# A gather of expert rows by one list of indices, and by two lists of which the second leaves out picks of weight zero

## The reference, cut to what matters

```python
PEER_TOPK = 16
...
        eidx = jnp.take_along_axis(cand_idx, pos, axis=-1)
        g = jax.nn.softmax(best, axis=-1)
        u = jnp.take(expert_u, eidx, axis=0)
        h = jax.nn.gelu(jnp.einsum('thkd,td->thk', u, xb))
        vv = jnp.take(expert_v, eidx, axis=0)
        return jnp.einsum('thk,thkd->td', (g * h.astype(jnp.float32)).astype(xb.dtype), vv)
```

## Time and profile before

| | |
|---|---|
| median of 3 runs | 3214.2 us (3211.79 to 3214.63) |
| span of the profiled execution, first to last instruction | 3210.9 us |
| instructions | 43682 |
| read from HBM | 1051.58 MB, 332 GB/s over the span |
| first gather starts | at 1816.18 us |
| last gather starts | at 3175.11 us |
| start of the last store | at 3205.95 us |

### The profile page before, as it was taken

One profiled execution on the slowest core, in us unless ns is written; L12 is line 12 of the kernel. 1 busy time (PEld: TensorE's weight loads), 2 busy tenths in 40 slices (PEclk: granted clock), 3 DMA queues, 4 the chain that ended last, 5 costly groups with the idle time before them and its releaser, 6 DMA issues.

```text
span 3210.9 us, 43682 instructions
## 1 busy us (share of the span) xinstructions
PE 2530.9 (79%) x17242; PEld 1248.3 (39%) x17242; DVE 1564.1 (49%) x3391; ACT 1048.7 (33%) x2457; POOL 581.5 (18%) x535
## 2 busy tenths in 40 slices
PE   8999988797988878878879878897778655555655
PEld 6677774484322222222228634343324211111111
DVE  4655655763100100100107466678675777777764
ACT  2533443521000000000006354577344444343433
POOL 0000000000000000000000143344443444444442
PEclk9999998998999999999999989898888777788778
DMA  4211302249999999999995499999999999999997
GB/s 152 101 58 66 122 26 112 92 158 382 427 427 427 427 427 427 427 427 427 427 411 195 176 418 399 417 418 383 420 419 420 420 420 419 420 419 420 420 419 331
DMA packets 128670, 1067.80 MB, mean 333 GB/s; under 512 B 14289, under 2 KB 17233, under 8 KB 27601
## 3 DMA queue, kind: packets, MB, share of 16 engines
q0 software_dynamic: 75456, 543.20, 41.0%
q1 hardware_dynamic: 53008, 521.81, 39.4%
HBM read 1051.58 MB, written 13.37 MB: 332 GB/s over the span
## 4 chain that ended last, share of the span: by engine, by line
DMA 50%; PE 34%; DVE 7%; ACT 6%; issue 2%; POOL 1%; ACTq 0%; DVEq 0%; SPq 0%; POOLq 0%
PE ps L92 33%; DMA gb<-in_peer_uv,eidx 27%; DMA gw<-in_eu 14%; DMA gw<-in_ed 8%; DVE gb L146 2%; PE ps L97 2%; ACT L168 1%; ACT dots L168 1%; ACT diag L168 1%; ACT prob L168 1%; POOL gb L86 1%; DVE prob L146 0%; DVE w_lo L115 0%; ACT prob_t L168 0%; DVE prob L120 0%
## 5 line engine op out<-in xcount | busy, mean ns | idle before, releaser
L92 PE MATMUL ps<-gb,diag 64*64 64x512 f32 x4096 | 662.0, 759 | 410.3 <-ACT diag L168 396.8
L146 DVE CUSTOM_DVE_ANT_0 gb<-gb,xn 128x1024 f32<-128x1024 f32 x512 | 627.1, 1225 | 378.5 <-DMA gb<-in_peer_uv,eidx 378.0
L86 POOL DMA_INDIRECT gb<-in_peer_uv,eidx x512 | 570.3, 1114 | 1312.6 <-PE ps L92 718.5
L92 PEld LDWEIGHTS ps<-gb,diag 64*64 64x64 f32 x4096 | 148.2, 155 | 847.6 <-ACT diag L168 746.3
L168 ACT ACTIVATE dots<-dots 128x1 f32<-128x1 f32 (+1 forms) x382 | 77.6, 203 | 618.3 <-DVE dots L146 611.5
L115 DVE TENSOR_TENSOR expert_act<-expert_act,ps 128x512 f32<-128x512 f32 x32 | 22.0, 687 | 523.8 <-PE ps L92 523.2
L92 PE MATMUL ps<-ga,xt 128*64 128x512 f32 x1024 | 229.2, 596 | 41.3 <-DMA ga<-in_eu 32.6
L92 PE MATMUL ps<-gw,xt 128*64 128x512 f32 x992 | 224.3, 601 | 25.4 <-DMA gw<-in_eu 16.2
L168 ACT ACTIVATE diag<-cons,dots 128x128 f32<-128x128 f32 x512 | 205.5, 401 | 41.1 <-ACT dots L168 0.4
L115 DVE TENSOR_TENSOR x<-x,ps 128x512 f32<-128x512 f32 (+1 forms) x96 | 61.4, 643 | 296.5 <-PE ps L92 294.9
L168 ACT ACT_TABLE_LOAD x124 | 159.1, 1283 | 8.1 <-PEq L3241 0.7
(11 more groups left out here) (360 smaller groups left out, 3616.9 us busy)
## 6 DMA issues: line engine op xcount, KB each, us to landing
ga<-in_eu SPq DMA_DIRECT2D x47, 2048.0 KB, 35.5
gw<-in_eg SPq DMA_DIRECT2D x46, 2048.0 KB, 30.7
ring<-in_wt SPq DMA_DIRECT2D x75, 1024.0 KB, 6.0
gw<-in_ed SPq DMA_DIRECT2D x32, 2048.0 KB, 35.5
ga<-in_ed SPq DMA_DIRECT2D x32, 2048.0 KB, 36.1
ga<-in_eg SPq DMA_DIRECT2D x17, 2048.0 KB, 32.2
gw<-in_eu SPq DMA_DIRECT2D x16, 2048.0 KB, 35.5
p_scratch<-spill SPq DMA_DIRECT2D x35, 256.0 KB, 2.1
```

Source lines behind the costliest of these rows:

```text
L86: self.e.indirect_dma_start(out, None, table, bass.IndirectOffsetOnAxis(ap=idx, axis=0)).then_inc(s, 16)
L92: i = self.e.matmul(out, l, r, start=st, stop=sp, skip_group_check=True)
L146: self.done(self.e.tensor_tensor_reduce(out=o, in0=a, in1=b, scale=scale, scalar=start, op0=o0, op1=o1, accum_out=acc), name)
```

## The change

Rows 256 to 495 are now of two kinds. A row is **whole**, as before, where n % 4 is 0 or 2 and n is not 256 or 384. The other 122 rows are **split**: a first gather fetches only u (4 KB for each partition) from the table seen as 32768 rows of 1024 floats, and a second one fetches only v, with an index that is known after the dot. 113 of the 122 second gathers have an upper bound on the index: DVE adds 65536 to the index of a pick whose dot is -11 or less, and the gather skips indices above 32767. DVE also sets the softmax weight of such a pick to zero, so what lies in the buffer does not count. The first nine second gathers (rows 256 to 271, quads 64 to 67) fetch all.

- The unit of the order is a **quad** of four rows, n = 4g to 4g + 3. After the four dots of a quad come (event "k") three small DVE instructions, `far`, `v_idx` and `mask`, then one gelu of four columns on ACT.
- POOL's order is: the u or whole gathers of quad g + 1 (four), then the v gathers of quad g (two), and so on.
- The sums of a quad's whole rows come during the dots of the next quad, the sums of its split rows one quad later (`sums_after`). "out" and "add" follow the order of the sums.
- Nine buffers are cut in halves: a u half is free after its dot, a v half after its sum. Four buffers (`KEPT`) are for whole rows. From row 496 on (`TAIL`) the 13 buffers are whole again.
- For blocks 2 and 3 the indices are doubled (`dv.ts(sif, siu, 2.0, MUL)`) and halved again for whole rows, one more small DVE instruction for each of 16 heads.

```diff
@@ Engine.gather
-        self.e.indirect_dma_start(out, None, table, bass.IndirectOffsetOnAxis(ap=idx, axis=0)).then_inc(s, 16)
+        if last is None:
+            self.e.indirect_dma_start(out, None, table, at).then_inc(s, 16)
+        else:
+            self.e.indirect_dma_start(out, None, table, at, bounds_check=last, oob_is_err=False).then_inc(s, 16)
@@ block_program
+    STEPS, GROW, ADD_LAG, HALVED, WHOLE, LAST = 27, 244, 2, 256, 496, 504
+    NO_GELU, FAR = -11.0, 65536.0
+    halves = I["peer_uv"].rearrange("e (t d) -> (e t) d", t=2)
+    def whole(n):
+        return n < HALVED or n % 4 in (0, 2) and n % 128 != 0 or n >= WHOLE
...
+    KEEP = sorted(range(len(ROW_BUFFERS)), key=lambda s: first_last[s])[:4]
+    PAIRED = [s for s in range(len(ROW_BUFFERS)) if s not in KEEP]
...
+    def sums_after(n):
+        if n < HALVED:
+            return list(row_group(n)) if n == row_group(n)[-1] else []
+        if n >= LAST:
+            k = n - LAST
+            return [[500, 501], [502, 503], [504, 505], [506, 507]][k] if k < 4 else [n]
+        g, j = n // 4, n % 4
+        before = [m for m in quad(g - 1) if whole(m)] if g > HALVED // 4 else []
+        later = [m for m in quad(g - 2) if not whole(m)] if g > HALVED // 4 + 1 else []
+        todo = later + before if g % 32 == 1 or g > WHOLE // 4 else before + later
+        return todo[j * len(todo) // 4:(j + 1) * len(todo) // 4]
@@ peer_order
+            yield ("u", n)
+            if n == group[-1]:
+                yield ("k", group)
+            for m in sums_after(n):
+                yield ("w", m)
+                q = SUM_AT[m]
+                if q == LAST - 1 or q % 128 == 127 and q < LAST:
+                    yield ("out", q // 128)
+                if 127 < q < LAST and q % 128 == ADD_LAG:
+                    yield ("add", q // 128 - 1)
@@ dv_peer
+            elif ev[0] == "k" and HALVED <= ev[1][0] < WHOLE:
...
+                if gated(n // 4):
+                    s4 = soft[:, i % 2, k:k + 4]
+                    dv.wait_ge(("inv", i, k // 16))
+                    dv.ts(far, d, NO_GELU, ALU.is_le, FAR, MUL)
+                    dv.stt(e, far, 1.0, e, ADD, ADD, name=("v_idx", n // 4))
+                    dv.stt(s4, d, NO_GELU, s4, ALU.is_gt, MUL, name=("mask", n // 4))
@@ po_peer
+        def v_row(n):
+            i, k = n // 128, n % 128
+            s, freed, _ = V_AT[n]
+            po.wait_ge(("v_idx", n // 4))
+            po.wait_ge(freed)
+            po.gather(v_of(n), halves, eidx[i % 2][:, k:k + 1], f"gv{s}", ("v_row", n), 2 * 16384 - 1 if gated(n // 4) else None)
+        for n in range(HALVED + 4):
+            u_row(n)
+        for g in range(HALVED // 4, WHOLE // 4):
+            for n in quad(g + 1):
+                u_row(n)
+            for n in quad(g):
+                if not whole(n):
+                    v_row(n)
+        for n in range(WHOLE + 4, 512):
+            u_row(n)
```

More of the change, by code:

```diff
@@ new lines, in quad, with places @@
+    def quad(g):
+        return range(4 * g, 4 * g + 4)
+    def places(rows, pieces, end, start=None):
+        held, out = list(start or [None] * len(pieces)), {}
+        for n in rows:
+            s = min((held[s] is not None, held[s] if held[s] is not None else s, s)
+                    for s, (_, first, _) in enumerate(pieces) if n >= first)[2]
+            freed = pieces[s][2] if held[s] is None else ("sum", held[s]) if held[s] < HALVED else (end, held[s])
+            out[n] = (s, freed, held[s] is None or held[s] < HALVED)
+            held[s] = n
+        return out, held
@@ new lines, in block_program @@
+    FIRST_AT, first_last = places(range(HALVED), ROW_BUFFERS, "sum")
+    KEEP = sorted(range(len(ROW_BUFFERS)), key=lambda s: first_last[s])[:4]
+    PAIRED = [s for s in range(len(ROW_BUFFERS)) if s not in KEEP]
+    KEPT = [(ROW_BUFFERS[s][0], 0, None) for s in KEEP]
+    U_PIECES = [(ROW_BUFFERS[s][0][:, 0:1024], 0, None) for s in PAIRED]
+    V_PIECES = [(ROW_BUFFERS[s][0][:, 1024:2048], 0, None) for s in PAIRED]
+    SPLIT = [n for n in range(512) if not whole(n)]
+    U_AT, u_last = places(SPLIT, U_PIECES, "dot", [first_last[s] for s in PAIRED])
@@ new lines, in u_of, with v_of, gated @@
+    def u_of(n):
+        return row_at(n)[0][:, 0:1024] if whole(n) else U_PIECES[U_AT[n][0]][0]
+    def v_of(n):
+        return row_at(n)[0][:, 1024:2048] if whole(n) else V_PIECES[V_AT[n][0]][0]
+    def gated(g):
+        return HALVED // 4 <= g < WHOLE // 4 and not any(V_AT[n][2] for n in quad(g) if not whole(n))
+    def row_group(n):
+        if n < GROW or n >= LAST:
+            return (n,)
+        if n < HALVED:
+            return (n - n % 2, n - n % 2 + 1)
+        return tuple(quad(n // 4))
@@ L2786, in peer_order @@
+    SUMS = [m for n in range(512) for m in sums_after(n)]
+    assert sorted(SUMS) == list(range(512)) and all(a // 128 <= b // 128 for a, b in zip(SUMS, SUMS[1:]))
+    SUM_AT = {m: q for q, m in enumerate(SUMS)}
+    ROW_ENDS = [SUMS[127], SUMS[255], SUMS[383], LAST - 1]
+    assert SUMS[LAST - 1] == LAST - 1
     def peer_order():
@@ L2810, in peer_order @@
                 done += 1
[L2811 to L2819, removed]
+            yield ("u", n)
[8 more added lines that the diff above has]
+                    yield ("add", q // 128 - 1)
+                if q == LAST + ADD_LAG:
+                    yield ("add", 3)
             if n - 3 in pass_rows:
```

148 lines of the change are left out of this document (88 added, 60 removed).

## The result

| | before | changed |
|---|---|---|
| median | 3213.6 us (3211.8 to 3214.6) | 3238.7 us (3235.2 to 3247.6) |
| ratio, 95% interval | 1 | **1.0083** (1.0068 to 1.0097) |
| span of the profiled execution | 3210.9 us | 3236.3 us |
| bytes in the DMA queues | 1067.8 MB | 1042.1 MB |

The change makes the kernel 0.8% slower (both measured again, on one chip). The forecast was 3196 us and faster; the range of 3176 to 3240 holds the result at its upper end.

The account below looks back on a forecast made before the run. DMA was taken to bound the kernel, with POOL next. Quads -38.6, block changes +15.6, first quads +0.7 and end +4.0 sum to -18.3 us: span 3192.6, time 3196 us; range 3176 to 3240.

Parts of the forecast that it names:

- The bound before: Before the change, the gathers' DMA queue sets the pace: 9.99 us per four rows, about ten gathers always queued.
- The saving in bytes, and the floor: In 56 bounded quads, 6282 skipped picks (26 MB) bring DMA's floor from 9.99 to 9.06 us, worth 52 us.
- the third rival: A skipped pick costs the engines as much as a fetched one: 10.15 us a quad, 3243 us; chance 0.07.
- POOL: Gathers begun in a dot wait for its end; quad taken as 9.3 us, between 9.06 and 9.64, gaining 38.6 us.
- The 9.64 us of the rival: POOL sets the quad's pace, each of four dots holding one gather 0.55 us: 3215 us; chance 0.19.
- the 78% that I set as its sign: If POOL leads, it is over 78% busy in the middle of block 2, with hardly any wait for DVE.
- There is slack, but of 1.4 us: After a quad's last u lands, the next whole row's bytes can begin at 8.9 us; the queue runs dry at 10.3.
- The two changes of block: Rows 266 and 394 wait for buffers whose sums stand behind the add; DMA stalls 2 x 7.8 = 15.6 us.
- The end: Block 3's "out" comes at row 505, not 503, with eight sums behind it: 4 us later (0 to 5).
- The slower rival: Bounded gathers take 0.2 us more each on POOL, which is the bound: 10.04 us a quad, 3237 us; chance 0.21.
- The fourth rival: Dots are also held by gathers, 0.47 us each: with the choice's long steps 9.6 us a quad, 3213 us; chance 0.03.
- What was to show it: Signs in the trace: 26 MB less read, GB/s and POOL's share in block 2, gather means, stalls near rows 266 and 394.

Follow-up runs that it names:

- b1: Kernel before the change, with dots of rows 256 on over 512 of 1024 columns: 3214.9 us, ratio 1.0000 to the kernel before.
- e7b: Changed kernel with five whole-row buffers, early add, dots over 512 columns from row 256 and threshold -7.8: 3167.0 us, 0.9848 of the kernel before.
- e8: Changed kernel with five whole-row buffers and early add, all picks of the bounded gathers fetched (FAR = 0): 3223.8 us, 1.0028 of the kernel before.
- e3: Changed kernel with five whole-row buffers instead of four, and the add at a new block's first sum instead of third: 3185.1 us, 0.9915 of the kernel before.
- e9: Changed kernel with five whole-row buffers and early add, all picks of the 113 bounded gathers skipped: 3177.5 us, 0.9889 of the kernel before.
- e5b: Changed kernel with five whole-row buffers instead of four, add left at the third sum: 3194.2 us, 0.9936 of the kernel before.
- e1: Changed kernel with FAR = 0, so all picks of the bounded gathers are fetched: 3247.3 us, 1.0104 of the kernel before.

## Why the prediction was wrong

- **The bound before.** Right: the gathers' queue led, and short dots gave nothing (b1). The quad was 10.12 us by the dots' starts, not 9.99, or 0.12 more; the rate of the window (420 GB/s) counts the small transfers of the other queue too.
- **The saving in bytes, and the floor.** Right. 25.7 MB of 26, and all 6282 picks; the floor of 9.06 us a quad was measured at 9.15 to 9.26 (e7b), and a quad with all fetched in six gathers at 10.19 (e8) where the third rival's sum had 10.15. One bound is off in the sums: a quad of 9.5 us gives 3207 us, not 3209.
- **POOL.** The mechanism was right, and the value chosen wrong. A gather that begins in a dot ends after it, by 0.81 to 0.82 us without a bound and 0.87 with one. In the changed kernel 150 of the 288 gathers of 2600 to 3100 us begin in a dot, before it was 85 of 197, and the means are 1.20 and 1.17 us, not the 1.10 of the earlier trace rows that pulled my choice towards the floor. 6 x (1.19 + 0.30) = 8.9 us are POOL's own. The 9.64 us of the rival (7.44 without any meeting, and four holds of 0.55) came close to what a kernel led by POOL takes, 9.48 in e3 and 9.50 in e9 over the 50 quads, but partly by luck: in e3 the holds come to 1.5 us and not 2.2, and waits of 0.5, which the sum did not have, make up for them. In e3 POOL was busy 76% of the time, so the 78% that I set as its sign was too high.
- **The failed step: "There is slack, but of 1.4 us".** The chain from dots to gathers was counted from the dots to the v gathers and "then the first whole row", as if that row's buffer were free. It was not: with four buffers for whole rows POOL waited for their sums, about 1 us per quad, and in series with the holds. 8.9 + 1.0 + 0.3 = 10.2 us instead of 9.3. I had named this place ("it is used up when ...") but only for the rare steps, Exp's table and the choice, and took the way from a dot's end to the release from the earlier trace rows, 2.5 us; in the changed kernel the sum alone ended 5.4 us (median) after the last dot. The index to POOL's gather, 0.8 us at the least, was put at nothing too. The 50 measured quads were to give 34.5 us (0.69 each) and cost 3.4, which is 37.9 of the 43.7 us between forecast and result, or 0.76 a quad: 0.70 for the buffers (10.18 to 9.48 with the fifth), 0.18 for the value chosen for POOL (9.48 for 9.3), less 0.12 for the quad before. That the buffers are the cause is shown by e5b, which changes only how the 13 buffers are shared out, one more for whole rows and one pair of halves less.
- **The two changes of block.** Right in place, mechanism and size: 15.6 us forecast and 0.7 for the first quads, 17.6 measured for both together, in pieces whose other six quads were to give 4.1 back, which the quads of this kernel don't. The waits of 12.4 (row 266) and 11.9 us (row 394) stand where they were to stand. I did not then ask what moving the add would bring, which is 14 us.
- **The end.** 4.0 us forecast, 0.8 measured from the last dot to the first add behind it, and 1.9 more between rows 495 and 511.
- **The slower rival.** The time (3237 us) came out by luck, its mechanism did not. In e8, where nothing holds them, bounded gathers took 1.00 us, 0.94 for the old form: 0.06 more, not 0.2, and 113 times that is 7 us where POOL leads. The fourth rival rested on a rule: by the Trainium skill, "SBUF — State Buffer", section "Who interferes with whom", a dot that comes second would be held as well. The 277 dots of the changed kernel that began inside a gather took 1.22 us in the mean like all the others, and so it was in the other runs with full dots: the traces don't bear that half out.
- **What was to show it.** "If bytes fall and GB/s falls with them, the chain or POOL is the bound": so it was. POOL was at 68 to 71%. The other sign, 26 MB less in the figure of 1051.58 MB, failed although the bytes fell; by its words the skip would have done nothing.

## What to carry to other kernels

When a long queue of independent transfers becomes a loop in which each transfer waits for a result, count the loop through every buffer it needs, not only through the data: the time that each release adds is in series with the engine's own time. After a cut in bytes that brings nothing, first shorten the loop (one more buffer, an earlier release), then measure the bytes again: the same skip was worth 0.1 us a quad in the loop (e1 to the changed kernel), 0.7 with the fifth buffer and the early add (e8 to e3), and 1.0 where short dots left DMA in the lead (e8 to e7b). An infrequent step, such as an add at a change of block, is free only as long as the queue behind it is deeper than the step's chain.

## What the runs showed of the hardware

- A queue's busy share is not its work. The same 3.74 MB a quad occupied the engines 10.14 x 0.965 = 9.8 us in the changed kernel and 9.26 x 1.009 = 9.3 us in e7b. And e3 stood at 99.5% though POOL set its pace.
- A skipped index appears as a packet of 4 bytes, which takes 9 ns where one of 4 KB takes 159; by the quads' times (e8, e7b) it costs the engines about a tenth of a fetched row. The "HBM read" of the page is 1051.58 MB with and without the skips.
- The gather with a bound takes 1.00 us of POOL, the one without 0.94 to 0.95.
- A gather begun in a dot ends 0.81 to 0.82 us after the dot does (median), in the kernel before as in all the changed ones, and one with a bound 0.87; the dot takes 1.22 to 1.23 us whether it begins inside a gather or not.
- The first gather that waits for an index from DVE begins 0.8 us or more after the instruction that writes it; one that waits for a sum of PE began 0.28 to 0.31 us after its end in 32 of 39 cases.
